# Two convolution taps and one copy moved to other steps in a hybrid DeltaNet block

## The reference, cut to what matters

```
xn = rms_norm(h);  q,k,v,z,b,a,sc_c,sc_u,sc_b,gate_a,gate_b = split(xn @ w_in)
q,k,v = silu(causal_conv4(q,k,v));  q,k l2-normalised;  beta, g from b, a
o   = chunk_gated_delta_rule(q,k,v,g,beta)        # 8 heads, chunks of 64
y_a = (rms_norm(o) * silu(z)) @ w_dn_out
y_b = (sc_b * causal_conv3(sc_c * sc_u)) @ w_sc_out
h   = h + (sigmoid(gate_a)*y_a + sigmoid(gate_b)*y_b) @ w_o
out = rms_norm(h + (silu(gt)*up) @ w_down),  gt,up = rms_norm(h) @ w_gate_up
```

## Time and profile before

| | us |
|---|---|
| Timed runs, median (lowest to highest) | 1136.91 (1135.36 to 1139.97) |
| The profiled execution | 1139.7 |
| Its span | 1137.9 |
| TensorE busy in it | 1104.8 |
| VectorE, ScalarE, GpSimd busy | 406.6, 470.4, 569.3 |

### The profile page before, as it was taken

How to read it: one execution, slowest core, us unless ns; L and a number is a source line. 1 busy time by engine, 2 the same in 40 slices (tenths; PEclk the granted TensorE clock), 3 DMA queues, 4 the chain that set the end, 5 groups by cost and what they waited for, 6 DMA issues and landing times.

```text
span 1137.9 us, 20480 instructions
## 1 busy us (share of the span) xinstructions
PE 1104.8 (97%) x8363; PEld 936.6 (82%) x8363; DVE 406.6 (36%) x635; ACT 470.4 (41%) x1009; POOL 569.3 (50%) x502
## 2 busy tenths in 40 slices
PE   7999999999999999999999999999999999999996
PEld 7899899898989898996878888878888888888884
DVE  6364847557574748474100011322111111100002
ACT  5554646364645546462422322443322222232221
POOL 4364535445364535354354555565555555554552
PEclk8999999999999999998999999999999999999998
DMA  4212111112111121111243232322322222233221
GB/s 174 75 57 75 57 57 57 58 56 77 56 57 57 57 75 57 57 57 57 74 169 102 82 111 79 101 98 93 93 93 93 93 93 93 93 103 99 94 75 74
DMA packets 26621, 93.28 MB, mean 82 GB/s; under 512 B 2848, under 2 KB 3104, under 8 KB 26528
## 3 DMA queue, kind: packets, MB, share of 16 engines
q1 hardware_dynamic: 25488, 89.88, 23.9%
q10 hardware_dynamic: 1040, 2.10, 0.5%
HBM read 89.87 MB, written 2.10 MB: 81 GB/s over the span
## 4 chain that ended last, share of the span: by engine, by line
PE 81%; DVE 10%; ACT 5%; issue 4%; POOL 1%; DVEq 0%; ACTq 0%; POOLq 0%
PE bank L1060 81%; DVE cv L952 4%; DVE am L772 1%; DVE xt L772 1%; ACT L743 1%; ACT w_hi L495 1%; DVE cv L976 0%; DVE xd L940 0%; ACT xd L499 0%; DVE qkv L787 0%; DVE raw L772 0%; DVE h L1053 0%; POOL w_lo L389 0%; DVE vb L772 0%; ACT nwt L605 0%
## 5 line engine op out<-in xcount | busy, mean ns | idle before, releaser
L389 POOL TENSOR_TENSOR w_lo<-w_raw,w_hi 128x512 fp32r<-128x512 f32 x324 | 424.9, 1329 | 521.6 <-ACT w_hi L495 521.3
L1060 PE MATMUL bank<-x_hi,w_hi 128*128 128x264 f32 (+1 forms) x896 | 252.2, 340 | 3.6 <-DVE x_lo L791 3.1
L1060 PE MATMUL bank<-x_lo,w_hi 128*128 128x264 f32 (+1 forms) x896 | 234.3, 320 | 0.0
L1060 PE MATMUL bank<-x_hi,w_lo 128*128 128x264 f32 (+1 forms) x896 | 233.3, 319 | 0.0
L495 ACT ACTIVATE w_hi<-w_raw 128x512 fp32r<-128x512 f32 x324 | 187.9, 622 | 107.0 <-PE bank L1060 106.7
L1060 PEld LDWEIGHTS bank<-x_hi,w_hi 128*128 128x128 f32 x896 | 149.5, 192 | 18.9 <-issue 3.6
L1060 PE MATMUL bank<-og_hi,w_hi 128*128 128x512 f32 x416 | 164.7, 396 | 0.0
L1060 PE MATMUL bank<-og_hi,w_lo 128*128 128x512 f32 x416 | 164.3, 395 | 0.0
L1060 PE MATMUL bank<-og_lo,w_hi 128*128 128x512 f32 x416 | 164.3, 395 | 0.0
L1060 PEld LDWEIGHTS bank<-x_hi,w_lo 128*128 128x128 f32 x896 | 150.1, 192 | 11.5
L1060 PEld LDWEIGHTS bank<-x_lo,w_hi 128*128 128x128 f32 x896 | 150.4, 192 | 8.6
(11 more groups left out here) (254 smaller groups left out, 1353.9 us busy)
## 6 DMA issues: line engine op xcount, KB each, us to landing
w_raw<-w_stream SPq DMA_DIRECT2D x162, 512.0 KB, 3.3
h_in<-h_t SPq DMA_DIRECT2D x4, 528.0 KB, 5.0
h<-h_t ACTq DMA_DIRECT2D x1, 2048.0 KB, 10.0
out<-h SPq DMA_DIRECT2D x8, 256.0 KB, 2.2
cst<-consts SPq DMA_DIRECT2D x1, 512.0 KB, 8.1
sm<-small SPq DMA_DIRECT2D x1, 80.5 KB, 6.1
wba<-w_ba SPq DMA_DIRECT2D x1, 64.0 KB, 7.3
```

The source lines that it names most:

```text
L389: nc.gpsimd.tensor_tensor(w_lo[:, n % 2, at], w_raw[:, n % 3, at], w_hi[:, n % 2, at].bitcast(f32), ALU.subtract).then_inc(wlo_ready, 1)
L1060: return nc.tensor.matmul(o, w, x, start=start, stop=stop)
```

## The change

VectorE's two taps of u's convolution leave the evacuation of u and become the beginning of the evacuation of b. They are issued in quarters 0 and 1 of the iteration behind b, behind steps 4 and 5, and the product for yb in quarter 2, behind step 6. On ScalarE the evacuation of b pauses for two more quarters, so that yb_hi is copied in quarter 3, behind step 7 and behind both halves of the next block's w_hi. GpSimd, TensorE and the queue are not edited.

```diff
@@ scalar, evacuate @@
                     inverse_root(rs2[:, :], dbank[0][:, :], 1.0 / D, 0).then_inc(rs2_ready, 1)
                 yield
+                if kind == "b":
+                    yield
+                    yield
                 if kind in ("b", "dn"):
                     i = m if kind == "b" else KT + m
                     act.wait_ge(yb_ready, i + 1)
@@ vector, evacuate @@
                     mult(raw[:, c % 2, 3 + HALF:3 + L], p[1][:, 0:HALF], cbuf[:, HALF:L]).then_inc(c_used, 1)
+                if kind == "b":
+                    c = conv_number("u", m)
                     dve.wait_ge(c_used, m + 1)
+                    yield from convolve(c, 1, sm[:, CSC + 3 * m:CSC + 3 * m + 3])
                     yield
-                    yield from convolve(c, 1, sm[:, CSC + 3 * m:CSC + 3 * m + 3])
-                if kind == "b":
                     if m:
                         dve.wait_ge(yblo_ready, m)
                     dve.wait_ge(conv_ready, 4 * m + 4)
```

## The result

The changed kernel takes 1117.39 us (median of four runs, 1117.20 to 1117.51); the kernel before, with one more run, 1137.55 (1135.36 to 1139.97). The ratio is 0.9821, with a 95% interval of 0.9804 to 0.9839. The forecast was 1117.2 in a range of 1113 to 1123. The runs before lay 4.6 us apart, those after 0.3.

A forecast was written before the change was run, and what follows sets the result against it. TensorE bounds the kernel (81% of the last chain), losing time to waits for VectorE's um update and clock falls behind them. From 1139.7 us, -15.9 - 7.0 + 0.4 = -22.5 gives 1117.2 us, range 1113 to 1123.

The forecast's parts named there:

- The holes: TensorE's waits for VectorE's update of um (line 883), in heads 1 to 7, vanish: 7 x 2.27 us, -15.9 us.
- The distance between the same operation of two heads: Sign in the profile after: head periods of about 59.7 us (61.9 - 2.27 + 0.05) between the same instructions.
- The clock: TensorE's granted clock no longer falls at or behind the waits of heads 1, 2, 6 and 7: -7.0 us.
- rival A: The clock falls anyway and only TensorE's waits for um go: 1124.2 us; chance 6%.
- Where the taps land: First tap issued 0.30 us before GpSimd's stretch ends; second through 0.46 us before the next block's w_lo.
- Rival B: Second tap is caught behind GpSimd's two w_lo, 2.2 us in each of eight heads: 1146 us, slower; chance 4%.
- rival C: Gain given back late in the head by a new 2.27 us wait: 1132.7 us or no change; chance 5%.
- The new wait for yb: TensorE's block after next waits 0.05 us a head for VectorE's later yb product, eight heads: +0.4 us.
- yb_hi and yb_lo: Later copies on ScalarE and GpSimd delay nothing: 0; if that cover failed, one copy of 0.63 us in one head.
- The sum: -15.9 - 7.0 + 0.4 = -22.5 us against the profiled execution of 1139.7 us, so 1117.2 us.
- stands until GpSimd rests: A VectorE tap with two large SBUF inputs ends only after GpSimd's gapless stretch, 0.57 us later; first tap took 5.32 us.
- the case that I gave 1%: By the skill's rule a caught second tap waits for one w_lo only, yb 0.9 us late a head: 1124 us; 1%.

The follow-up runs named there:

- Two experiments: Kernel before with GpSimd's product qdec cut to 8 columns: 1124.83 us; changed kernel with both taps and the yb product one quarter later: 1124.98 us.
- port kernels: Three kernels without the block, GpSimd's stretch against one VectorE tap: taps 0.73 to 1.73 us, at most 2.52, then 4.99 to 5.73 behind 16-partition products, else 0.72 to 1.30.

## Why the prediction was right, point by point

- **The holes, -15.9 us.** Right. The second level follows its predecessor after 0.33 us, and the list no longer has the wait. The distance between the same operation of two heads was forecast at about 59.7 us and is 59.70 and 59.69 (VectorE's timeline, raw, start to start, heads 3 to 5):

```profile
252.69 0.75 DVE L775 TENSOR_TENSOR raw<-bank,cbuf 128x264 f32<-128x264 f32 x2
...
312.39 0.75 DVE L775 TENSOR_TENSOR raw<-bank,cbuf 128x264 f32<-128x264 f32 x2
...
372.08 0.75 DVE L775 TENSOR_TENSOR raw<-bank,cbuf 128x264 f32<-128x264 f32 x2
```

- **The clock, -7.0 us.** Right: none of the five windows is left, and rival A (1124.2, the clock falls anyway) is out. Two experiments happened to land on that number for another reason, eight or seven holes of 1 us. The spread of before's runs was put down to the number of falls; after the change, with none in the heads, it shrank from 4.6 to 0.3 us. The 36 runs of the kernel before that stand beside the experiments fit too: those under 1135.6 us have a mean granted clock of 0.992 to 0.994, those over 1139 one of 0.985 to 0.988, and most lie near 1135.3, 1136.7, 1138.2 or 1139.7, steps of about the 1.45 us of one fall. Why the clock falls behind four of seven equal holes, and behind which, no run shows.
- **Where the taps land.** The first was forecast to wait 0.30 us, and the second to be through 0.46 us ahead of w_lo. They are: start 318.23, GpSimd's last mask until 318.55, both ended at 319.92, w_lo at 320.29, so 0.37 us ahead. Rival B (caught behind w_lo) is out. So is rival C (the gain given back later in the head): the list has no new wait.
- **The new wait for yb, +0.4 us.** Right to the hundredth in the trace: 0.44 us where 0.39 are needed, in a block that was forecast to be 0.05 late, and 0.45 us over the eight heads. Being one quarter later costs 1.04 us a head, 0.90 expected.
- **yb_hi and yb_lo, 0.** Right; GpSimd makes yb_lo from 324.40, 3.70 us behind step 6's start (forecast 3.8). The step that I undersold is that the move of yb_hi is no mere consequence. VectorE's half without it is 12 us slower than before, which I had worked out only for the experiment.
- **The sum.** Up to block sc 0, the end of the affected stretch, the forecast was -22.5. It starts at 502.10 now and started at 524.64, so -22.54. The span lost 22.2. The remaining 0.3 us are a pace that differs from one execution to the next: between 580 and 710 us two blocks mostly take 11.17 to 11.18 us in the trace of before and 11.20 in that of after. The kernels do not decide it: the changed kernel run again has 11.17 there, and the kernel before with ScalarE's half alone 11.20.
- **What was wrong** is a reason, not a term. The prediction says that a tap "stands until GpSimd rests". That holds only behind narrow products, and with tiny masks not even there. The rule of the Trainium skill ("SBUF — State Buffer", section "Who interferes with whom": the port is held for one instruction) is what 20 of 20 taps did without them, and 20 of 20 did not with them; and in the block, with the products on 128 partitions, the hole is gone, as the prediction said it would be by that rule. The number did not suffer, because the changed kernel's first tap comes while the last mask of the stretch runs, where both rules give the same end. The price of rival B was too high for the same reason: ahead of those two w_lo stands idle time and no narrow product, so by the port kernels a caught tap would have waited for one of them, the case that I gave 1%. In this place it was not run.

  That a tap does not always stand until GpSimd rests could have been seen in the trace of before, in the head without a hole. Head 0's second tap came during a w_lo (75.69) and got in at its end, ahead of a mask that followed without a gap. So the prediction was wrong that "the trace does not bear that rule out":

```profile
75.69 1.28 POOL L389 TENSOR_TENSOR w_lo<-w_raw,w_hi 128x512 fp32r<-128x512 f32 x1
...
75.78 1.76 DVE L952 SCALAR_TENSOR_TENSOR cv<-raw,sm,cv 128x528 f32<-128x528 f32 x1
...
76.93 1.18 POOL L375 TENSOR_TENSOR alev<-am,cst 128x256 f32<-128x256 f32 x1
```

## What to carry to other kernels

A short operation that takes seven times its usual time (5.32 us instead of 0.76) is worth a look at the other engines: look what ends a fixed time before it does, here 0.57 us. Before moving it out of the way, look also at heads or iterations of the same program in which it is short, and for what makes the other engine hold on; here widening five tiny products from 16 to 128 partitions bought the same 1.8% as reordering two engines. When a result is moved later, move every instruction that waits for it in another engine's queue behind the work that does not.

## What the runs showed that I had not expected

- GpSimd instructions on 16 partitions, two of them with a wait between, then a run of wide ones without a gap: the VectorE operation with two SBUF inputs gets no turn until the run ends (4.99 to 5.73 us in 20 trials, 5.28 to 5.33 in the seven heads). The exception is the kernel with masks of 8 columns, where it got in after three instructions in seven heads (2.12 to 2.15 us); why is open. With 128 partitions, or a gap (head 0 of the kernel before, where GpSimd idles 0.37 us ahead of its first w_lo and the first tap took 0.73), it gets in at the next boundary. Why the width matters was not measured.
- The waits between the narrow products seem to matter too: behind five without a wait a tap missed at most one boundary, behind two with and three without it missed all. That compares two port kernels; none was run that differs in the waits alone. The waits by themselves do nothing: with them and 128 partitions every tap was short.
- Holes of 0.9 to 1.2 us left the granted clock at 2.4 GHz in 7 and in 8 heads. Of seven holes of 2.3 us four were followed by 1.2 GHz, in the kernel before as with ScalarE's half alone, and of eight of 2.6 us six.
